# Five projection products moved into three other norms, and smaller first transfers, in a two-block transformer kernel

## The reference

```
for i in 0, 1:
    h = layer_norm(ALPHA*h + 0.5*swiglu(h, ffn[i,0]))       # norms "ffn0", "ffn2"
    h = layer_norm(ALPHA*h + mixer_i(h))                    # norms "ab", "c"
    h = layer_norm(ALPHA*h + 0.5*swiglu(h, ffn[i,1]))       # norms "ffn1", "ffn3"
    h = h + (p[i] @ ple_w_proj[i]) * sigmoid(h @ ple_w_gate[i])
```

## Time and profile before

| | us |
|---|---|
| median of three runs | 2883.22 (2882.93 to 2883.66) |
| the profiled execution, its own time | 2883.02 |
| its span, first to last instruction | 2881.2 |
| TensorE busy | 2797.4 |
| VectorE busy | 1770.6 |
| ScalarE busy | 623.7 |
| GpSimd busy | 315.0 |

### The profile page before, as it was taken

How to read it: one execution, slowest core, us unless ns; L and a number is a source line. 1 busy time by engine, 2 the same in 40 slices (tenths; PEclk the granted TensorE clock), 3 DMA queues, 4 the chain that set the end, 5 groups by cost and what they waited for, 6 DMA issues and landing times.

```text
span 2881.2 us, 34220 instructions
## 1 busy us (share of the span) xinstructions
PE 2797.4 (97%) x13390; PEld 2145.7 (74%) x13390; DVE 1770.6 (61%) x3753; ACT 623.7 (22%) x1360; POOL 315.0 (11%) x301
## 2 busy tenths in 40 slices
PE   9999999999999999999999899999999999999985
PEld 6888886668888877888864587888877766885321
DVE  4788688785766475566358766677356445664223
ACT  1322121022221022221022412222022464001001
POOL 0000020020000100000101430000201373001221
PEclk9999999999999999999999999999999999999998
DMA  4223433121322222132211111232222201257998
GB/s 170 117 103 124 131 122 121 48 77 78 117 88 103 88 88 88 60 117 103 102 62 59 44 59 66 88 117 91 100 74 95 103 16 59 88 223 286 424 424 329
DMA packets 62885, 349.51 MB, mean 121 GB/s; under 512 B 8174, under 2 KB 14446, under 8 KB 23936
## 3 DMA queue, kind: packets, MB, share of 16 engines
q1 hardware_dynamic: 45792, 320.88, 29.1%
q10 hardware_dynamic: 12064, 17.98, 1.8%
q0 software_dynamic: 4864, 8.40, 0.8%
HBM read 337.79 MB, written 14.16 MB: 122 GB/s over the span
## 4 chain that ended last, share of the span: by engine, by line
PE 89%; DVE 4%; DMA 3%; SPq 2%; ACT 1%; issue 1%; POOL 0%; ACTq 0%; DVEq 0%; POOLq 0%
PE bank L927 33%; PE bank L1125 31%; PE bank L538 6%; PE bank L547 5%; SPq L3882 2%; PE bank L3944 2%; DMA ring<-in_weights 2%; PE bank L2785 2%; PE bank L576 2%; PE bank L3370 2%; PE bank L2769 1%; PE bank L3963 1%; PE bank L568 1%; PE bank L3007 0%; PE bank L672 0%
## 5 line engine op out<-in xcount | busy, mean ns | idle before, releaser
L927 PE MATMUL bank<-area,mixed 128*128 128x256 f32 x2264 | 508.4, 379 | 2.4 <-DVE mixed L949 1.8
L927 PEld LDWEIGHTS bank<-area,mixed 128*128 128x128 f32 x2264 | 429.6, 190 | 62.2 <-DVE mixed L949 2.5
L927 PE MATMUL bank<-area,ring 128*128 128x256 f32 x1536 | 346.3, 379 | 0.1
L1125 PE MATMUL bank<-area 128*128 128x256 f32 x1440 | 323.9, 379 | 0.0
L927 PEld LDWEIGHTS bank<-area,ring 128*128 128x128 f32 x1536 | 291.4, 190 | 40.3 <-DVE area L968 0.5
L1125 PEld LDWEIGHTS bank<-area 128*128 128x128 f32 x1440 | 273.6, 190 | 37.2
L1125 PE MATMUL bank<-buf_b,area 128*128 128x256 f32 x1040 | 239.3, 379 | 0.0
L1125 PE MATMUL bank<-buf_a,area 128*128 128x256 f32 x1040 | 239.1, 379 | 0.0
L1125 PEld LDWEIGHTS bank<-buf_b,area 128*128 128x128 f32 x1040 | 197.5, 190 | 27.1 <-issue 0.3
L1125 PEld LDWEIGHTS bank<-buf_a,area 128*128 128x128 f32 x1040 | 197.6, 190 | 26.9
L949 DVE TENSOR_TENSOR mixed<-ring 128x512 f32<-128x512 f32 (+2 forms) x95 | 65.0, 684 | 223.1 <-PE bank L927 222.8
(11 more groups left out here) (641 smaller groups left out, 4355.6 us busy)
## 6 DMA issues: line engine op xcount, KB each, us to landing
ring<-in_weights SPq DMA_DIRECT2D x236, 1024.0 KB, 4.8
area<-in_weights SPq DMA_DIRECT2D x35, 1024.0 KB, 27.8
buf_b<-in_weights SPq DMA_DIRECT2D x10, 1024.0 KB, 26.5
buf_a<-in_weights SPq DMA_DIRECT2D x8, 1024.0 KB, 25.1
const<-in_weights SPq DMA_DIRECT2D x5, 1024.0 KB, 27.7
norm<-in_weights SPq DMA_DIRECT2D x4, 1024.0 KB, 23.0
mixed<-in_weights SPq DMA_DIRECT2D x4, 1024.0 KB, 27.2
area<-area ACTq DMA_DIRECT2D x20, 128.0 KB, 2.4
```

The costliest lines, as they stand in the source:

```text
L927: mm = pe.e.matmul(b, w[:, k * P:(k + 1) * P], x(INPUT_OF[p], unit.lo + k), start=(unit.key, BANK_OF[p]) not in begun, stop=unit.last and ...
L1125: mm = pe.e.matmul(out[:, half * H:(half + 1) * H], weights[:, at:at + P], x(name, d), start=fresh and half == 0 and d == 0, stop=half == ...
```

## The change

- Of the eight projections of layer 0, product 0 stands in ab's norm before the scales and product 1 behind them; six stay in ffn1's norm, one before the scales and five behind. Of layer 1, products 0 and 1 stand in ffn2's norm, product 2 in c's norm behind the scales, and five stay in ffn3's norm, one before the scales and four behind. They take the place of the idle products there.
- Their weights move in the packing: 512 columns to the place ahead of ffn1's lead, 512 ahead of c's index products, 256 ahead of ffn3's lead.
- The early results are kept in two free stretches of `area` and in `stat`. p moves to another stretch that the wide parts overwrite, so it is loaded four times: in ab, and behind the wide part of ffn1, ffn2 and ffn3. VectorE waits, ahead of the wide sums, for the last early product that read it.
- x chunk 0 and the first 512 columns of block 0 are transfers of their own, with their own semaphores (shared with later uses, whose counts are raised); chunk 4 and the other 1536 columns follow. Four idle products at the start in place of eight.

```diff
@@ -163,20 +163,23 @@
...
     plan["ab_out"] = thin_pieces("ab_w_out", (0,), HALVES)
+    plan["ple0_early"] = dense("ple_w_proj", (0,), PLE, 0, 2 * P)
     plan["ffn1_lead"], plan["ffn1_wide"] = lead_pieces(0, 1), wide_pieces(0, 1)
...
-    plan["ple0_proj"] = dense("ple_w_proj", (0,), PLE, 0, D)
+    plan["ple0_proj"] = dense("ple_w_proj", (0,), PLE, 2 * P, D - 2 * P)
...
     plan["ffn2_down"] = ffn_pieces(1, 0)
+    plan["ple1_early"] = dense("ple_w_proj", (1,), PLE, 0, 2 * P)
     plan["c_index"] = (dense("c_w_in", (0,), D, AI, IH * ID) +
...
     plan["c_out"] = thin_pieces("c_w_out", (0,), NEXT)
+    plan["ple1_third"] = dense("ple_w_proj", (1,), PLE, 2 * P, P)
     plan["ffn3_lead"], plan["ffn3_wide"] = lead_pieces(1, 1), wide_pieces(1, 1)
...
-    plan["ple1_proj"] = dense("ple_w_proj", (1,), PLE, 0, D)
+    plan["ple1_proj"] = dense("ple_w_proj", (1,), PLE, 3 * P, D - 3 * P)
@@ -495,6 +501,8 @@
...
+    FIRST_COLUMNS = LEAD["ffn0_lead"] * P
+
@@ -502,7 +510,9 @@
...
         block, col = places[stream.at]
         stream.at += 1
-        if block != stream.block:
+        if block == 0 and col < FIRST_COLUMNS:
+            pe.wait_ge(first_weights, 16)
+        elif block != stream.block:
             stream.block = block
             pe.wait_ge(block_loaded[block % RING], 16 * (block // RING + 1))
@@ -586,9 +596,9 @@
...
-    BESIDE, IDLE_ROOT, IDLE_SCALE, IDLE_RMS = ("ffn1", "ffn3"), 6, 6, 3
+    IDLE_ROOT, IDLE_SCALE, IDLE_RMS = 6, 6, 3
     IDLE_RANK, IDLE_SLOTS, IDLE_ROWS = 10, 8, 5
-    IDLE_FIRST = 8
+    IDLE_FIRST = 4
@@ -627,22 +637,31 @@
...
-    def plan_mean(st, beside=None):
+    SPREAD_TO = {"ab": (0, 0, 1), "ffn2": (1, 0, 1), "c": (1, None, 2)}
+    BEFORE_SCALES = 1
+
+    def plan_mean(st, beside=()):
 
         i = NORMS.index(st)
         order = [(g.turn + j) % 8 for j in range(8)]
         g.add(("mean", st), (mean_read, i + 1))
         g.add(("squares", st), (square_read, STATS[st] + 1))
         g.add(("means", st), (means_read, i + 1))
-        if beside is None:
+        if st in SPREAD_TO:
+            layer, first, second = SPREAD_TO[st]
+            if first is not None:
+                plan_ple_proj(layer, first, order[0])
+            plan_scales(st)
+            plan_ple_proj(layer, second, order[1])
+            return
+        if not beside:
             plan_scales(st)
             return
-        others = itertools.cycle(order[4:] + order[:2])
-        for m in range(KD):
-            if m == KD // 2:
+        for n, ((layer, m), b) in enumerate(zip(beside, order[4:] + order[:2])):
+            if n == BEFORE_SCALES:
                 plan_scales(st, order[3])
-            beside(m, next(others))
-        g.turn = next(others)
+            plan_ple_proj(layer, m, b)
+        g.turn = order[4]
 
@@ -679,7 +698,7 @@
...
-    def tensor_stats(pe, st, r, ready):
+    def tensor_stats(pe, st, r, ready, beside=None):
...
         end(g, mm, ("squares", st))
         pe.wait_ge(mean_read, i + 1)
         spread(pe, ("means", st), mean_c)
-        if st not in BESIDE:
+        if beside:
+            beside()
+        else:
             idle_products(pe, ("squares", st), (square_read, STATS[st] + 1), IDLE_ROOT)
 
-    def tensor_scales(pe, st):
+    def tensor_scales(pe, st, beside=None):
         pe.wait_ge(inverted, STATS[st] + 1)
         spread(pe, ("scales", st), scale_c)
-        if st not in BESIDE:
+        if beside:
+            beside()
+        else:
             idle_products(pe, ("squares", st), (square_read, STATS[st] + 1), IDLE_RMS if st in RMS else IDLE_SCALE)
@@ -1675,6 +1698,8 @@
...
         if i == 0:
             scalar_s5_load(ac)
+        else:
+            scalar_load_p(ac, (i - 1) // 2 + (i == 2))
         for k in range(KD):
@@ -1689,8 +1714,12 @@
...
+    P_READ_BY = {1: ("proj", 0, 1), 2: ("proj", 0, KD - 1), 3: ("proj", 1, 2)}
+
     def vector_wide_up(ve, i, h, r, ready, beside=None):
         vector_wide_inputs(ve, i, h, r, ready)
+        if i in P_READ_BY:
+            ve.wait_ge(*g.done(P_READ_BY[i]))
         for p in range(AHEAD):
             vector_wide_sums(ve, i, 0, p)
@@ -1974,7 +2003,21 @@
...
-    pt, proj = chunks(region(81 * H, 2 * T), 2), chunks(region(BASE + 2 * T, KD * T), KD)
+    pt, proj = chunks(region(86 * H, 2 * T), 2), chunks(region(BASE + 2 * T, KD * T), KD)
+    early_proj = region(81 * H, T), region(83 * H, T), stat[:, :]
+    PROJ_PLAN = ((("ple0_early", 2), ("ple0_proj", 6)), (("ple1_early", 2), ("ple1_third", 1), ("ple1_proj", 5)))
+    P_LOADS = {"ple0_early": 1, "ple0_proj": 2, "ple1_early": 3, "ple1_third": 3, "ple1_proj": 4}
+    N_EARLY = 2, 3
+
+    def proj_weights(layer, m):
+
+        for name, n in PROJ_PLAN[layer]:
+            if m < n:
+                return name, m
+            m -= n
+
+    def projected(layer, m):
+        return early_proj[m] if m < N_EARLY[layer] else proj[:, m, :]
@@ -1990,17 +2033,18 @@
...
     def plan_ple_proj(layer, m, bank):
-        g.add(("proj", layer, m), (proj_done, KD * layer + m + 1), blocks=B(f"ple{layer}_proj", m), bank=bank)
+        g.add(("proj", layer, m), (proj_done, KD * layer + m + 1), blocks=B(*proj_weights(layer, m)), bank=bank)
 
     def tensor_ple_proj(pe, stream, layer, ms):
-        pe.wait_ge(p_loaded, 16 * (layer + 1))
         for m in ms:
-            product(pe, stream, g, ("proj", layer, m), plan[f"ple{layer}_proj"][m], cols(pt))
+            name, n = proj_weights(layer, m)
+            pe.wait_ge(p_loaded, 16 * P_LOADS[name])
+            product(pe, stream, g, ("proj", layer, m), plan[name][n], cols(pt))
...
-            ac.e.activation(proj[:, m, :], bank(("proj", layer, m)), ACT.Copy).then_inc(proj_done, 1)
+            ac.e.activation(projected(layer, m), bank(("proj", layer, m)), ACT.Copy).then_inc(proj_done, 1)
@@ -2038,7 +2082,7 @@
...
-            ve.step(tt(gate_of(m), gate_of(m), proj[:, m, :], ALU.mult))
+            ve.step(tt(gate_of(m), gate_of(m), projected(layer, m), ALU.mult))
@@ -2530,6 +2574,8 @@
...
+        ac.wait_ge(*g.done(("y", KC - 1)))
+        scalar_load_p(ac, 0)
         ac.wait_ge(z_done, KC)
@@ -4224,14 +4270,14 @@
...
-    plan_mean("ffn1", lambda m, b: plan_ple_proj(0, m, b))
+    plan_mean("ffn1", [(0, m) for m in range(N_EARLY[0], KD)])
...
-    plan_mean("ffn3", lambda m, b: plan_ple_proj(1, m, b))
+    plan_mean("ffn3", [(1, m) for m in range(N_EARLY[1], KD)])
@@ -4247,7 +4293,7 @@
...
     def x_ready(k):
-        return x_loaded[k % (KD // 2)], 16
+        return (first_x if k == 0 else x_loaded[k % (KD // 2)]), 16
@@ -4267,30 +4313,30 @@
...
+
+        def projections(layer, first, last):
+            return lambda: tensor_ple_proj(pe, s, layer, range(first, last))
+
         tensor_first_idle(pe)
         tensor_wide_ffn(pe, s, 0, buf_a, buf_b, x_ready)
         tensor_stats(pe, "ffn0", buf_b, ffn_ready(0))
         tensor_scales(pe, "ffn0")
         tensor_ab(pe, s, buf_a, ln_ready("ffn0"))
-        tensor_stats(pe, "ab", buf_b, ab_ready)
-        tensor_scales(pe, "ab")
+        tensor_stats(pe, "ab", buf_b, ab_ready, projections(0, 0, 1))
+        tensor_scales(pe, "ab", projections(0, 1, 2))
         tensor_wide_ffn(pe, s, 1, buf_a, buf_b, ln_ready("ab"))
-        tensor_stats(pe, "ffn1", buf_b, ffn_ready(1))
-        tensor_ple_proj(pe, s, 0, range(0, 4))
-        tensor_scales(pe, "ffn1")
-        tensor_ple_proj(pe, s, 0, range(4, KD))
+        tensor_stats(pe, "ffn1", buf_b, ffn_ready(1), projections(0, N_EARLY[0], N_EARLY[0] + BEFORE_SCALES))
+        tensor_scales(pe, "ffn1", projections(0, N_EARLY[0] + BEFORE_SCALES, KD))
         tensor_ple(pe, s, 0, buf_a, ln_ready("ffn1"))
         tensor_wide_ffn(pe, s, 2, buf_b, buf_a, ple_ready(0))
-        tensor_stats(pe, "ffn2", buf_a, ffn_ready(2))
-        tensor_scales(pe, "ffn2")
+        tensor_stats(pe, "ffn2", buf_a, ffn_ready(2), projections(1, 0, 1))
+        tensor_scales(pe, "ffn2", projections(1, 1, 2))
         tensor_c(pe, s, buf_b, ln_ready("ffn2"))
         tensor_stats(pe, "c", buf_a, c_ready)
-        tensor_scales(pe, "c")
+        tensor_scales(pe, "c", projections(1, 2, 3))
         tensor_wide_ffn(pe, s, 3, buf_b, buf_a, ln_ready("c"))
-        tensor_stats(pe, "ffn3", buf_a, ffn_ready(3))
-        tensor_ple_proj(pe, s, 1, range(0, 4))
-        tensor_scales(pe, "ffn3")
-        tensor_ple_proj(pe, s, 1, range(4, KD))
+        tensor_stats(pe, "ffn3", buf_a, ffn_ready(3), projections(1, N_EARLY[1], N_EARLY[1] + BEFORE_SCALES))
@@ -4327,8 +4373,11 @@
...
-        for k in range(KD // 2):
-            ac.e.dma_start(buf_a[:, k::KD // 2, :], io["x"].rearrange("(c p) t -> p c t", p=P)[:, k::KD // 2, :]).then_inc(x_loaded[k], 16)
+        x_chunks = io["x"].rearrange("(c p) t -> p c t", p=P)
+        ac.e.dma_start(buf_a[:, 0, :], x_chunks[:, 0, :]).then_inc(first_x, 16)
+        ac.e.dma_start(buf_a[:, KD // 2, :], x_chunks[:, KD // 2, :]).then_inc(x_loaded[0], 16)
+        for k in range(1, KD // 2):
```

(57 more changed lines are left out.)

4 lines of the change are left out of this document (2 added, 2 removed).

## The result

| | before | after |
|---|---|---|
| median of ten runs, us | 2883.22 (2882.28 to 2885.99) | 2889.44 (2886.61 to 2892.84) |
| the profiled execution, its own time | 2883.02 | 2889.90 |
| its span | 2881.2 | 2888.0 |

The ratio is 1.0022, its interval 1.0014 to 1.003: slower by 6.2 us. I had said 2884.8 and a range up to 2888.6, so the time is 4.6 over the forecast and 0.8 over the range.

A forecast was written before the change was run, and what follows sets the result against it. TensorE was taken to bound the kernel, with 89% of the chain that ended last. Terms -2.25 - 3.35 - 4.2 + 2 x (4.05 + 1.70) = +1.7 gave 2884.8 us, range 2879.3 to 2888.6.

The forecast's parts named there:

- The blocks: Seam behind ffn1's and ffn3's leads: three-block leads make the fourth wide block late, stalling TensorE; +4.05 us each.
- The two norms: Projections taken out of ffn1's and ffn3's norms let the gates start earlier; -3.35 and -4.2 us.
- ab, ffn2, c and p's loads: Projections replacing idle products in these norms, and loading p four times, cost nothing; 0 each (norms 0 to +0.5).
- The start: Kernel start: small first transfers land at 4.75 instead of 7.41, less 0.4 for half speed; -2.25 us (0 to -3.1).
- The 0.52 MB wanted have moved at about 3.9: Kernel start: bytes of x chunk 0 and first weights, from early queue rates, moved by about 3.9 us.
- The upper bound, 7.41: Kernel start: latest time taken for the first real product, 7.41 us, meaning no gain.
- The lower bound: Kernel start: earliest landing, 4.24 us, from issue at 0.74 plus 3.5 for 512 KB with nothing else running.
- the estimate of 3.2: Kernel start: 3.2 us for 512 KB from the skill's fixed time and rate, 0.3 under the profile's 3.5.
- hidden, by about 1 us: Kernel start: second chunk and rest of the block, there by 7.41, are needed only at 8.6.
- the second half of the term: Kernel start: first real products run at half speed from 4.75 to 5.6, giving back 0.4 us.
- The clock behind the stalls: Behind ffn1's and ffn3's seam gaps the TensorE clock falls to half; +1.70 us twice (0 to 2.1 each).
- the rival by which the clock holds: Both seam stalls occur but the clock stays full; 3.4 us less, 2881.4, chance 0.20.

The follow-up runs named there:

- e1: The changed kernel with ffn1's and ffn3's leads each starting on a new block; 2878.72 us, 0.9983 of the kernel before.
- e9: The kernel before with 512 unused columns ahead of ffn1's and of ffn3's lead, nothing else of the change; 2897.46 us, ratio 1.0054 to before.
- e5: The changed kernel with the leads on a new block and the start of the kernel before put back; 2875.74 us, 0.9973 of before.
- e8: The changed kernel with both queues (SP, ACT) holding their second transfers until their first has landed; 2887.72 us, one run.
- e10: The changed kernel with leads on a new block and both queues holding second transfers until a VectorE memset ends; 2878.17 us, 0.9981 of before.
- e2: The changed kernel with eight idle products at the start again instead of four; 2888.80 us, 1.0019 of before.
- e4: The changed kernel with 31 small idle products inside the second wide product of ffn1 and ffn3, behind TensorE's wait; 2903.83 us, 1.0067 of before.
- e11: The changed kernel with SP alone holding its second transfer until the first weights have landed; 2891.58 us, one run.
- e12: The changed kernel with ACT alone holding its further transfers of x until chunk 0 has landed; 2885.58 us, one run.
- e7: The changed kernel with 15 small idle products between the first wide product and the wait in ffn1 and ffn3; 2886.15 us, 1.0009 of before.

## Why the prediction was wrong, point by point

- **The blocks: right.** The gaps are 3.87 and 4.00 where the terms were 4.05 each (the second product comes 4.03 and 4.18 later, counted from the first). e1 and e9 show that it is the packing. This part of the change, which its words don't speak of, decides its sign.
- **The two norms: right.** -3.24 for -3.35 and -4.08 for -4.2. The scales moved up by the 5.06 worked out; the unit that wants projection 6's bank was late by 0.77 instead of 0.85.
- **ab, ffn2, c and p's loads: right**, nothing: from the spread of the means to the next lead, ab's and c's norm take 0.1 less than before and ffn2's 0.1 more. In e5, which has all of them, the gain is the two norms'.
- **The start: wrong, and the step that failed.** "The 0.52 MB wanted have moved at about 3.9" counted all bytes of the first microseconds as the pair's. Chunk 4, the pairs of x and the rest of block 0 are issued from 1.19 on and take their share; the pair lands at 6.6 instead of 4.75, and only with both queues held back (e8, e10) does it come at 4.9. The upper bound, 7.41, was the nearer one. The lower bound rests on p's 3.5 us "when nothing else runs"; p is issued at 643.68, with SP's two blocks 0.85 behind it, and 3.5 was no guide to a start where several transfers are issued at once. Nor was the estimate of 3.2: the Trainium skill ("DMA: Bandwidth & Descriptors", Anatomy of one DMA) gives that fit for transfers that GpSimd issues, and these are ACT's and SP's. Chunk 4, which was to be "hidden, by about 1 us", would not have been: it lands 7.9 after its issue at 1.19, at 9.1, and the start as forecast wanted it at 8.6. Then the second half of the term: I had the first products at half speed up to 5.6, since I took TensorE to go on without a pause. It paused for 1.75 and stayed at half until between 10.30 and 11.00. The term was -2.25 (bounds -3.1 and 0, +1 with a half-speed group); it measured +1.34, 3.6 off, and +1.1 to +2.6 over the five traces that have this start.
- **The clock behind the stalls: right in kind, too small in size in ffn3.** 1.70 in ffn1, as in the forecast. ffn3 lost some 3.0 (7.14 less the 4.18), over the upper bound of 2.1. That is one outcome of two, and the forecast had the commoner one: seven traces have this gap with nothing to fill it (the changed kernel's, e2, e4, e8, e9, e11 and e12), and added up over the granted-clock rows ten of their fourteen seams lose 1.7 us and four lose 3.4, three in ffn3 and, in e11, one in ffn1. e7 shows that the fall hangs on TensorE standing still. The prediction drew on the Trainium skill ("TensorE: Matmul & The Clock Gate", What's actually happening), by which half speed is the default and activity lifts it. All fourteen seams agree: the clock falls at each, the gap is paid for twice, and the rival by which the clock holds is out.
- **Not forecast:** the falls that come and go. Before, the clock stays at 1.00 behind the wait of 2.77 that ends at 2184.23; after, behind the same wait, which ends at 2190.70, it is at 0.50 from 2192 on. In ffn0's norm, likewise, it is at 1.00 before and at 0.50 after. Each pair is before, then after; the rows of the first pair give TensorE alone and all engines:

```profile
2186.00:2188.00 2.00, 2.00 (x7) 1.00 0.00 0
2192.00:2195.00 3.00, 3.00 (x5) 1.35 (x4) 0.60 (x1) 2.63 (x4) 0.00 (x0) 0.50 0.03 11
...
414.00:417.00 3.00, 2.02 (x18) 1.83 (x17) 2.96 (x6) 0.00 (x0) 0.00 (x0) 1.00 0.00 0
414.00:417.00 3.00, 3.00 (x20) 2.68 (x13) 2.48 (x6) 1.30 (x2) 0.00 (x0) 0.50 0.18 74
```

Ten of the fourteen traces have the fall in ffn0's norm, the one before and three others don't. Such falls differ between two traces in code that the change didn't touch, so a pair of profiles agrees in a stretch to some 1.7 us at best.

The sum: 1.7 forecast, 6.8 in the spans; 3.6 of the difference is the start, 1.4 ffn3's clock, and the rest nearly cancels.

## What to carry to other kernels

Look at what a moved weight does to the packing: where a group begins decides which block is in the ring when, and 512 columns in front of a group that ends with all its blocks at once cost a whole transfer's latency, twice here. A small first transfer is early only if little is issued behind it, on its own queue too; and work taken away from a warm-up is only free if what it waited for really comes earlier. With half of it the lead took 1.7 us or more longer in nine of ten traces, part of that for a wait on transfers.

## What the runs showed of the hardware that I had not expected

- Transfers queued behind a small one on the same queue delay it: chunk 0 landed 5.5 after issue with ACT's further transfers and without SP's (e11, one trace), 4.2 without either (e8, e10). What in the queue does it was not settled.
- The clock can fall behind the gap, not in it: in e4 at 653.1 (0.43 of the row from 653 are lost), after 1.2 us of renewed work without a pause. Idle products behind the gap didn't prevent it (e4), those in the gap did (e7).
- Each of the fourteen gaps of 3.9 to 4.7 us met a fall, which lost 1.7 us in ten of them and 3.4 in four, both sizes at the same place in different traces. What makes the difference stays open.
- Behind the same wait of 2.77 us the clock held in one trace and fell in another (1.00 from 2186 before, 0.50 from 2192 after).
